# Looping VectorE's expert rows and gathering the last row's U rows in pairs, in a two-block transformer kernel

## The reference

```python
def peer_ffn(z, peer_wq, keys1, keys2, peer_u, peer_v):
    ...
    def chunk(zc):                                  # 128 tokens
        q = (zc @ peer_wq).astype(jnp.float32).reshape(PEER_CHUNK, PEER_HEADS, 2, PEER_HALF)
        s1 = jnp.einsum('chd,hkd->chk', q[:, :, 0], k1)
        s2 = jnp.einsum('chd,hkd->chk', q[:, :, 1], k2)
        v1, i1 = lax.top_k(s1, PEER_TOPK)           # 16 of 128 keys, twice
        v2, i2 = lax.top_k(s2, PEER_TOPK)
        ...
        top_s, top_pos = lax.top_k(cand, PEER_TOPK) # 16 of 16*16 sums
        expert = jnp.take_along_axis(cand_idx, top_pos, axis=-1)
        gate = jax.nn.softmax(top_s, axis=-1)
        u = jnp.take(peer_u, expert, axis=0)
        act = jax.nn.gelu(jnp.einsum('chkd,cd->chk', u, zc))
        v = jnp.take(peer_v, expert, axis=0)
        w = (gate * act.astype(jnp.float32)).astype(zc.dtype)
        return jnp.einsum('chk,chkd->cd', w, v).astype(zc.dtype)
```

## Time and profile before

| | before |
|---|---|
| time, median of 3 runs | 2484.34 us (2482.23 to 2484.65) |
| the profiled execution: its time, its span | 2483.83 us, 2482.0 us |
| busy: TensorE, VectorE, GpSimd, ScalarE | 86%, 61%, 29%, 28% |
| DMA, mean over the span | 305 GB/s, 756.68 MB |
| DMA queues: q0 (GpSimd), q1 (SyncE, ScalarE) | 540.12 MB, 215.28 MB |
| DMA queues that carry instructions: q8, q14 | 57 packets, 0.93 MB; 35 packets, 0.29 MB |

### The profile page before, as it was taken

The page is one execution under the profiler, slowest core; times in us unless marked ns, Lnnn a source line. Parts: engine busy times, 40 slices in busy tenths (PEclk is TensorE's granted clock), DMA queues, the critical chain, the costliest instruction groups (busy, mean ns, idle before and its releaser), DMA issues.

```text
span 2482.0 us, 32162 instructions
## 1 busy us (share of the span) xinstructions
PE 2133.8 (86%) x11988; PEld 1577.5 (64%) x11988; DVE 1505.8 (61%) x2166; ACT 694.4 (28%) x1159; POOL 718.6 (29%) x658
## 2 busy tenths in 40 slices
PE   7999999999999999999887767876687768776686
PEld 7999999999999999999833323332233223332232
DVE  5445665555646676767966555665555655655545
ACT  5435555544434445544211000100000000100001
POOL 3000000000002414121674444444344434444441
PEclk9999999999999999999898889988998889888998
DMA  9645454655666455565999999999999999999997
GB/s 275 212 144 154 152 154 151 193 180 179 216 213 205 152 164 170 167 206 196 404 422 421 421 422 422 421 422 422 421 422 422 422 421 422 422 421 422 422 422 298
DMA packets 281772, 756.68 MB, mean 305 GB/s; under 512 B 12160, under 2 KB 213328, under 8 KB 214992
## 3 DMA queue, kind: packets, MB, share of 16 engines
q0 software_dynamic: 74816, 540.12, 52.6%
q1 hardware_dynamic: 206624, 215.28, 27.8%
q10 hardware_dynamic: 240, 0.07, 0.0%
HBM read 752.26 MB, written 2.10 MB: 304 GB/s over the span
## 4 chain that ended last, share of the span: by engine, by line
PE 52%; DMA 35%; DVE 8%; issue 2%; POOL 2%; ACT 1%; ACTq 0%; DVEq 0%; POOLq 0%
PE PS L1769 40%; DMA RZ<-in_peer_u,idxu 18%; DMA RAW<-in_peer_u,idxu 16%; PE PS L2050 8%; DVE RZ L1615 2%; DVE RAW L1615 2%; DVE WL L1108 1%; POOL EX L637 1%; DMA EX<-in_peer_v,idxv 1%; PE PS L1899 1%; PE PS L1975 1%; DVE SM L1615 1%; PE PS L1875 0%; PE PS L1888 0%; PE PS L2014 0%
## 5 line engine op out<-in xcount | busy, mean ns | idle before, releaser
L2050 PE MATMUL PS<-EX,RK 128*128 128x512 f32 x1968 | 910.1, 617 | 312.7 <-ACT RK L1073 188.6
L2050 PEld LDWEIGHTS PS<-EX,RK 128*128 128x128 f32 x1968 | 378.5, 197 | 843.6 <-issue 710.8
L1769 PE MATMUL PS<-XH,WH 128*128 128x256 f32 x2832 | 782.8, 285 | 5.4 <-DVE SM L1203 2.4
L1769 PE MATMUL PS<-XH,WL 128*128 128x256 f32 x2832 | 776.9, 283 | 0.0
L1769 PE MATMUL PS<-XL,WH 128*128 128x256 f32 x2832 | 706.6, 283 | 0.0
L1108 DVE TENSOR_TENSOR WL<-RAW,WH 128x1024 fp32r<-128x1024 f32 x380 | 472.2, 1254 | 368.9 <-ACT WH L726 365.6
L1769 PEld LDWEIGHTS PS<-XH,WH 128*128 128x128 f32 x2832 | 544.4, 192 | 9.9 <-DVE WL L1108 5.4
L726 ACT ACTIVATE WH<-RAW 128x1024 fp32r<-128x1024 f32 x380 | 399.3, 1059 | 533.9 <-PE PS L1769 525.4
L1769 PEld LDWEIGHTS PS<-XH,WL 128*128 128x128 f32 x2832 | 544.5, 192 | 0.0
L1769 PEld LDWEIGHTS PS<-XL,WH 128*128 128x128 f32 x2832 | 502.3, 192 | 0.3
L1615 DVE CUSTOM_DVE_ANT_0 RZ<-RZ 128x2048 f32<-128x2048 f32 x126 | 288.8, 2292 | 249.2 <-DMA RZ<-in_peer_u,idxu 248.8
(11 more groups left out here) (339 smaller groups left out, 1273.4 us busy)
## 6 DMA issues: line engine op xcount, KB each, us to landing
RAW<-in_w_in SPq DMA_DIRECT2D x110, 1024.0 KB, 5.2
RAW<-in_w_out SPq DMA_DIRECT2D x32, 1024.0 KB, 5.6
RAW<-in_w_ple_gate SPq DMA_DIRECT2D x16, 1024.0 KB, 5.7
RAW<-in_peer_wq SPq DMA_DIRECT2D x16, 1024.0 KB, 6.3
RAW<-in_w_up_a SPq DMA_DIRECT2D x8, 1024.0 KB, 5.7
RAW<-in_w_up_b SPq DMA_DIRECT2D x8, 1024.0 KB, 5.7
EX<-in_peer_v,idxv POOLq DMA_INDIRECT x252, 26.5
RZ<-in_x SPq DMA_DIRECT2D x2, 1024.0 KB, 6.2
```

The source lines that it names most:

```text
L1769: ins = mm(o[:, t, :], left, right, start=(begins and k == t == m == 0), stop=(ends and k == QUARTER_KT - 1 and m == len(pairs) - 1), skip ...
L2050: ins = mm(bank(4 * (1 - hf) + c), left, right[:, 512 * c:512 * (c + 1)], start=False, stop=True, skip_group_check=True)
```

## The change

VectorE's rows 2 to 13 become two loops of three passes, each pass two rows: rows 2 to 7 for the first half of the tokens and rows 8 to 13 for the second. Row 14 and row 15 stay written out, as do rows 0 and 1. What is computed in them, and in which order, stays.

In GpSimd's last stage, the U rows of row 15 that are left (6 to 15) go two behind each of V(14,8) to V(14,12) in place of one behind each of ten V rows. U(15,8) and later wait for the multiply eight places ahead, which frees their slot; U(15,6) and U(15,7) wait for the last two multiplies of row 14. V(15,0) to V(15,7) follow behind V(14,15) with nothing between them.

```diff
@@ -689,13 +689,16 @@
-            for k in range(TOPK):
-                if k < 8:
-                    gather_v(ROWS - 2, 0, 8 + k)
-                else:
-                    gather_v(ROWS - 1, 1, k - 8)
-                if k < TOPK - U_AHEAD:
-                    gather_u(ROWS - 1, 1, U_AHEAD + k)
+            for k in range(8):
+                gather_v(ROWS - 2, 0, 8 + k)
+                for n in range(U_AHEAD + 2 * k, min(U_AHEAD + 2 * k + 2, TOPK)):
+                    if n >= U_SLOTS:
+                        g.wait_ge(S["u_used"], (ROWS - 1) * TOPK + (n + 1 - U_SLOTS))
+                    else:
+                        g.wait_ge(S["u_used"], (ROWS - 2) * TOPK + (n + 1 + U_SLOTS))
+                    gather(peer_u, ubuf[n % U_SLOTS], u_landed[n % U_SLOTS], idxu, 1, n)
+            for k in range(V_SLOTS):
+                gather_v(ROWS - 1, 1, k)
@@ -1694,8 +1697,13 @@
-            for r in range(2, ROWS - 1):
-                expert_row(r // PEER_HEADS, r, r % 2)
+            with v.Fori(1, PEER_HEADS // 2) as i:
+                for par in range(2):
+                    expert_row(0, i * 2 + par, par)
+            with v.Fori(PEER_HEADS // 2, ROWS // 2 - 1) as i:
+                for par in range(2):
+                    expert_row(1, i * 2 + par, par)
+            expert_row(1, ROWS - 2, 0)
```

## The result

The changed kernel takes 2488.2 us (median of 13 runs, 2486.0 to 2491.05) against 2483.7 (13 runs, 2482.23 to 2484.65) of the kernel before: a ratio of 1.0019 [1.0012, 1.0027]. It is 4.5 us slower where 5.2 us faster was forecast; the time lies inside the range of 2477 to 2490, in the upper part that rival 1 put there. The profiled execution took 2487.8 us, its span 2486.0.

The account below looks back on a forecast made before the run. It took the DMA engines, ending on one late engine, to bound the kernel. Six fewer code blocks, taken as 5.5 x 0.94 = 5.2 us, and 0 for the U order gave 2479.2 us; range 2477 to 2490.

Parts of the forecast that it names:

- rival 1: VectorE's loops: code blocks read again at the jump back, 0.94 us each, making it slower; chance 0.25 first loop, 0.12 both.
- What bounds the kernel: Second half, 16 expert rows: DMA engines bound it, share 1.01; one late engine sets every landing and the end.
- The price of a block: Landing chain: each 8 KB block of VectorE code read on q14 costs 0.94 us, bounds 0.32 and 1.0.
- Rival 2: The late DMA engine is late by itself, code blocks only coincide: 2483 to 2484.3 us; chance 0.12.
- The body's size: VectorE's loops: each body is 293 instructions or 2.3 blocks; 12 blocks read become 6 if bodies stay.
- Does a body stay?: VectorE's instruction store: a loop body stays over its passes, no repeated reads; bounds none to 20 blocks.
- rival 1's first case: Only VectorE's first loop reads 4 to 10 blocks again: 2483 to 2488.5 us, middle 2486; chance 0.25.
- What was costed at nothing: VectorE's rows: register instructions, 0 to 12 us a row, and a few us of stall at a jump, hidden by idle time.
- The U order: GpSimd's last stage: two U gathers for each V cost 0 us alone, bounds -1 and +3.
- it is needed for the other part: With the old U order, TensorE's row 15 backlog would lose some 4 us of landings coming 5 us sooner.
- Rival 3: Last rows: TensorE cools in gaps and products at 2425 to 2435 slow, 0 to 3 us, 2479 to 2482; chance 0.08.
- The tail: End of the kernel: the stretch at DMA share 0.06 shrinks from 9 us to 4 or 5.

Follow-up runs that it names:

- pad40w: The changed kernel with 40 instructions, each an already met wait, on VectorE ahead of its first loop: 2477.58 us, 0.9978 of the kernel before.
- after: The changed kernel itself, with VectorE's two loops and GpSimd's new order of U rows: 2488.2 us, 1.0019 of the kernel before.
- pad108w: The changed kernel with 108 instructions, each an already met wait, ahead of VectorE's first loop: 2488.51 us, 1.002 of the kernel before.
- more_code2: The kernel before with 128 already met waits on VectorE ahead of each of rows 2 to 13, all written out: 2496.66 us, ratio 1.005.
- pe_written: The kernel before with TensorE's rows 0 to 13 written out in place of its two loops: 2483.34 us, ratio 0.9997.
- u_order: The kernel before with only GpSimd's new order of the last U rows: 2484.48 us, ratio 1.0003.
- pad40w_old_u: The changed kernel with 40 already met waits ahead of VectorE's first loop, but the old U order: 2477.57 us, 0.9975 of the kernel before.

## Why the prediction was wrong, point by point

**What bounds the kernel** was right: DMA share 1.01 in every row of every kernel here, and the chain ends on the last gather's landing in all of them.

**The price of a block** was right, 0.94 us a trifle low. Packets on q14 from 1312 us (or the end of row 1) on, against the kernel before with its 16, and the difference of the medians:

| kernel | packets | more than before | us more | us a block |
|---|---|---|---|---|
| pad40w | 11 | -5 | -5.9 | 1.2 |
| after | 20 | +4 | +4.5 | 1.1 |
| pad108w | 21 | +5 | +5.1 | 1.0 |
| more_code2 | 28 | +12 | +13.2 | 1.1 |

The intervals of these ratios reach some 2 us to each side, so the rows say it more sharply. In pad40w, after and pad108w, rows 4 to 14 hold 6 fewer, 4 more and 5 more blocks than in the kernel before and take 5.8 us less, 3.9 and 4.9 more: 1.0 us a block each time. (pad40w's eleventh packet, at 2466 us, comes behind the last landing.) In more_code2 it is 11.1 us for 10 blocks, with the lower rate told above. Rival 2 is refuted by that run's rows 4 and 6.

Where the microsecond goes, the records of single DMA packets show. In the kernel before, from 1305 to 2445 us, q0 moves 58515 packets of 8 KB, and 0.31 us is the usual time of one. Only 20 take more than 0.4 us, and 20 instruction packets move in that time; each long packet begins within 0.02 us of the end of one of these. Twelve packets of q14, as many as the prediction counted for VectorE, take some 0.33 us, and the long one behind each takes 0.96 or 0.97: 0.33 + 0.97 - 0.31 makes 0.99 us. The records don't name the DMA engine, so that both are on the late one is read from the times. The four other packets of q14 have one of 0.66 to 0.69 us behind them. Two of these four lie in row 15, which takes 79.5 us, so they cost the landings nothing. The Trainium skill's DMA: Bandwidth & Descriptors, Latency and other measured facts, has two DMA engines usually slower, by its guess for another reason. No run here tells which engine is the late one, but the differences between these kernels go by VectorE's code.

**The body's size** was right: VectorE's records from one branch to the next number 292 in each of the six passes, 293 by the working. So was the sum of 12 blocks that become 6 without repeats, and that the first body would end a few instructions into a fourth block.

**"Does a body stay?" is the step that failed**, in its words "I take none, by TensorE's loop, the nearest row". That row was of another engine, whose blocks are 16 KB on a queue of their own (pe_written puts ten more on q8) and whose body of six is held; it says nothing of how many 8 KB blocks VectorE's store holds. Measured: a VectorE body that touches three blocks is read once (both loops of pad40w, one each of after and pad108w), and one that touches four is read again in each pass, five packets a pass (in after and in pad108w), which fits all four and the one ahead. The working had this number, 5 a pass, as its upper bound, and had counted the first body into its fourth block; with ten repeats rival 1's first case gives 2488.5, against 2488.2 measured. The Trainium skill's Runtime: NRT & Kernel Launch, Instruction fetch mechanics, has a store of 32 KiB for most engines but of 128 KiB for TensorE, and a stop at a branch whose target has left it. Worked out from its 32 KiB, four blocks of 8 KB, as an estimate, a body over three blocks stays with one read ahead and a body over four doesn't; the runs with loops agree, 0 and 5 packets a pass, with a stall of 5.5 to 5.8 us. The prediction had worked that case out too and gave it 0.25, against 0.43 for a forecast that rested on a row of another engine.

**What was costed at nothing** held. The stall at the jump is 5.5 to 5.8 us long and the DMA share in it 1.02. The 39 register updates a row are hidden: pad40w's looped rows take the 79.5 us of a written-out row without a block.

**The U order** costs and gives nothing alone, as forecast: 1.0003. In u_order too TensorE's wait of 12.40 us is gone, and its last wait of 0.93 is now 1.29. But "it is needed for the other part" was wrong. The error was to move the landings of V up by 5 us and leave TensorE's row 15 where it was. Row 15's start waits for weights that come from U landings, which the same late engine sets; all moves up together, and the margin stays (0.93, then 1.20).

**Rival 3** happened in its first half only: two products ran at the lower clock, 5.37 us each in place of 3.67, but with 2.07 and 2.09 us of waiting behind them no backlog came of it.

**The tail.** The stretch in which one DMA engine works alone was to shrink from 9 us to 4 or 5. In pad40w it is 4 to 5 us long, and in pad40w_old_u as well (stretch table, in turn):

```profile
2458.00:2462.00 4.00, 4.00 (x11) 1.66 (x9) 1.82 (x1) 0.00 (x0) 0.00 (x0) 1.00 0.06 27
...
2459.00:2463.00 4.00, 4.00 (x11) 1.71 (x9) 1.75 (x1) 0.00 (x0) 0.00 (x0) 1.00 0.08 33
```

But in u_order, which gains nothing, it also shrinks, to about 6 us (share 0.09 from 2463.7 to 2469.7), since the new order holds the other fifteen up. So this sign proves less than it seemed to.

**Left open.** Why the gather packet next to an instruction packet takes longer. And why 16 KB blocks of q8 cost nothing: in pe_written such a packet takes 1.0 to 1.1 us and the gather packet behind it 0.76 to 0.86 in place of 0.31, so each takes up some 1.5 us of a DMA engine. Either they go to engines with time to spare, or it is something else; no run here separates these.

## What to carry to other kernels

Before written-out code is made a loop, count the body's instructions (register updates too) and where its start lies in the engine's blocks; a body that touches one block too many reads all of them in every pass, which here turned a gain of 6 us into a loss of 4.5. A bound taken from another engine's loop is no evidence on the engine in question. Where one DMA engine ends late, the time goes by what that engine alone is given, however small; idle time of the other fifteen costs nothing while they still end first, as in u_order.

## What the runs showed of the hardware that was not expected

- Forty instructions that do nothing, ahead of a loop, took 10.6 us off the kernel (2488.2 to 2477.6).
- VectorE's blocks cost about 1.0 us per 8 KB, TensorE's nothing for 16 KB (pe_written, ratio 0.9997).
- An instruction packet slows the gather packet next to it: 0.97 us in place of 0.31 behind each of VectorE's 12 blocks in the kernel before. This, and not the block's own 0.33 us, is two thirds of its price.
- Where the code isn't held, VectorE stands for 5.5 to 5.8 us at the branch, though the packet itself takes 0.33 to 0.34 us. In the changed kernel the first three reads of the pass come at 1479, 1484 and 1489 us, 5 us apart, which is the 4.97 of a landing step; that each read waits for its turn among the gathers' packets is a guess that fits, not shown.
